# The backward half of the step-weighted C times B, moved from one VectorE multiply to four ScalarE copies per chunk

## The chip, the cores and the metric

The kernel runs on one core of one Trainium2 chip. The metric is the device time of one execution in microseconds (us). TensorE multiplies matrices, VectorE, ScalarE and GpSimd work on tiles in the on-chip memory SBUF and in TensorE's result banks, and the queues of SyncE, ScalarE and GpSimd issue DMA transfers. Each engine works its instructions in order, and engines wait for one another on semaphores.

## The reference

Two layers of a bidirectional encoder over 512 tokens of width 1024. The part that matters here is the Mamba-2 scan, in chunks of 128 tokens, once forward and once backward over the same x, B and C (8 groups, 4 heads each, state 128):

```python
def ssd_chunked(x, dt, A, Bm, Cm):
    ...
    X = (x * dt[..., None]).reshape(b, c, l, g, r, p)
    ...
    Lmat = jnp.exp(jnp.where(lower, seg, -jnp.inf))
    CB = jnp.einsum("bclgn,bcsgn->bcgls", Cc, Bc)
    y_diag = jnp.einsum("bcgrls,bcsgrp->bclgrp", CB[:, :, :, None] * Lmat, X)
    ...
    y_off = jnp.einsum("bclgn,bcgrpn->bclgrp", Cc, prev) * decay_out[..., None]
    return (y_diag + y_off).reshape(b, s, h, p)
...
    y_f = ssd_chunked(xs, dt_f, A[0], Bm, Cm)
    flip = lambda t: jnp.flip(t, axis=1)
    y_b = flip(ssd_chunked(flip(xs), flip(dt_b), A[1], flip(Bm), flip(Cm)))
    y = y_f + y_b + xs.astype(jnp.float32) * d_skip[:, None]
    y = y.reshape(b, s, D_INNER) * jax.nn.silu(z.astype(jnp.float32))
```

Around it stand a combined input projection, a Conformer convolution branch, gates, layer norms and a SwiGLU block, all of them large matrix products.

## The kernel before

Activations lie transposed, 128 features by 512 tokens. Every float32 product is made of three passes on TensorE, over a high and a low part of each operand (lines 855 to 857). All weights come as one stream of tiles of 512 KB in four slots. SyncE loads a tile to `raw`, ScalarE's `hi` (lines 466 and 467) writes its high part to `whi` and its negative to `wlo`, and GpSimd's `lo` (line 354) then issues a DMA that adds the tile itself to `wlo`; TensorE may use the slot when that has landed.

Each layer works its 8 groups in 4 pairs (`pair`), and then runs the dense stages. The order inside a pair is written out by hand, once for each engine. A pair begins with projections and ends with the output projection of its 512 inner features. Between these each of its two groups goes through its four chunks c = 0 to 3:

- GpSimd's `masked_steps` and TensorE's `exponent` make the exponents, ScalarE's `decay` (line 518, eight activations of 128x64) takes them through Exp to `E[:, c]`, forward and backward in one 128x128 matrix for each head.
- TensorE's `c_dot_b` makes C times B of all four chunks. VectorE's `mask_cb` (line 1313) writes it masked to `cb`, the upper and the lower triangle apart (FWD and BWD), and tells with `cb_done`.
- VectorE's `mix` (lines 1351 to 1359) weights `cb` with the steps dt of each head, backward and forward, in `tm`, and multiplies the sum into `E[:, c]`. It tells with `m_ready`.
- TensorE's `state` makes the chunk states, ScalarE's `state` (line 526) copies them to `H` in three parts, state 0, 1 and 2. VectorE's `entering` (lines 1324 and 1327) makes the entering states of them by four carries and four gains; its fourth instruction waits for state 2 (`st_evac`). It tells with `h_ready`.
- ScalarE's `skip` (line 510) starts `y` with x times D.
- TensorE's `y_chunk` multiplies `E[:, c]` with x (line 971), and then, behind the wait for `h_ready`, the states with C (line 977). For chunks 2 and 3 it first waits until VectorE's `outputs` of chunk 0 or 1 has read the banks (line 1379, `yp_read`). `outputs` ends with the gate (line 1383).
- ScalarE's `square`, GpSimd's `group_rms` and VectorE's `normalise_y` (line 1390) normalise y, TensorE's `y_transpose` (line 988) turns it.

Order of VectorE in the second group: `mix` of chunks 0 and 1, `entering`, `mix` 2, `outputs` 0, `mix` 3, `outputs` 1 to 3. TensorE's order behind it: chunk 3 of `y_chunk`, the output projection's first six k-steps (line 855 with `y_hi`; the fifth and sixth use weight slot 1), and then `y_transpose`.

Of the kernel before, what the change touches and what calls it, by code (L numbers as in the profile page):

```python
# [100 lines left out]
def on(cyc, n):  # L101

    return cyc[0] + n, cyc[1] + n


def build(nc, x_in, p_in, w_stream, w_dt, w_ple, par_in, out):
    ctx = ExitStack()
    with ctx:
        def sb(name, shape, dtype=F32, where=None):
            return (where or ctx).enter_context(nc.sbuf_tensor(name, shape, dtype))  # L110

        def sem(name):
            return ctx.enter_context(nc.semaphore(name))
# [27 lines left out]
        with ExitStack() as r:  # L141
            cin = sb("conv_in", [P, 4, T], F32, r)
            feat = sb("xs_b_c", [P, 4, T], F32, r)
            xtok = sb("x_tok", [P, CH, GW], F32, r)
            btok = sb("b_tok", [P, CH, STATE], F32, r)
            ztok = sb("z_tok", [P, 2, T], F32, r)
            E = sb("decay", [P, CH, HG, P], F32, r)
            rhs = sb("seg_rhs", [P, 2, 2 * HG, HB], F32R, r)
            cb = sb("cb_masked", [P, 2, CH, P], F32, r)
            xw = sb("x_weighted", [P, 2, 2, GW], F32, r)  # L150
            H = sb("states", [P, CH * 2, GW], F32, r)
            y = sb("y_tok", [P, CH, GW], F32, r)
            tm = sb("tmp_m", [P, HG, P], F32, r)
            ty = sb("tmp_y", [P, 2, GW], F32, r)
            junk = sb("squares", [P, GW], F32, r)
        with ExitStack() as r:
# [31 lines left out]
        ident = sb("ident", [P, P])  # L188
        par = sb("params", [P, NPAR])
        stepf = steps[:, :, :, :, :].rearrange("p k d c h -> p k (d c h)")  # L190
        tmf = tm[:, :, :].rearrange("p a b -> p (a b)")
        tyf = ty[:, :, :].rearrange("p a b -> p (a b)")
        swap = E[:, 1, 0, :]
        nega = E[:, 1, 1, 0:2 * HEADS]
# [51 lines left out]
        st_done = sem("st_done")  # L246
        st_evac = sem("st_evac")
        h_ready = sem("h_ready")
        m_ready = sem("m_ready")
        yo_done = sem("yo_done")  # L250
        xd_ready = sem("xd_ready")
# [51 lines left out]
        def seen(n):  # L303

            return n + EARLY
# [5 lines left out]
        def open_(e, *ss):  # L311
            for s in ss:
                e.sem_inc(s, EARLY)
# [139 lines left out]

        @block.scalar
        def _(act):
            open_(act, xh_done, silu_done, tok_evac, xd_ready, exp_done, st_evac, ss_done, yh_done,
                  sq_ready, std_ready, zf_ready, zh_ready, bh_done, fh_done,
                  square_ready, off_sq_ready, diag_ready, gate_ready, e_evac, esq_ready, estd_ready, dt_evac, dt_e, cum_exp, nega_e,
                  dtw_hi, *hi_done)
# [29 lines left out]
            def silu(G, c):  # L489
                act.wait_ge(conv_done, seen(4 * G + c + 1))  # L490
                act.activation(feat[:, c, :], feat[:, c, :], ACT.Silu).then_inc(silu_done, 1)
# [12 lines left out]
            def skip(g, G):  # L504

                act.wait_ge(tok_evac, seen(3 * G + 2))
                act.wait_ge(yt_done, seen(2 * G))
                for h in range(HG):
                    e = slice(h * HEAD, (h + 1) * HEAD)
                    i = act.activation(y[:, :, e], xtok[:, :, e], ACT.Copy, scale=par[:, O_DSK + g * HG + h:O_DSK + g * HG + h + 1])  # L510
                i.then_inc(xd_ready, 1)

            def decay(g, G, c):
                act.wait_ge(seg_done, seen(CH * G + c + 1))
                for h in range(HG):
                    for half in range(2):
                        t = slice(half * HB, (half + 1) * HB)
                        i = act.activation(E[:, c, h, t], quarters(bank[4 + c % 2])[:, h, t], ACT.Exp,  # L518
                                           bias=of(EDGE, half, c, g)[:, h:h + 1])
                i.then_inc(exp_done, 1)  # L520

            def state(G, n):

                act.wait_ge(st_done, seen(3 * G + n + 1))
                dst = (H[:, 3:5, :], H[:, 0:6:5, :], H[:, 2:8:5, :])[n]
                act.activation(dst, halves(bank[6 + n % 2]), ACT.Copy).then_inc(st_evac, 1)
# [79 lines left out]
            def pair(L, base, j, first=False):  # L606

                c0 = (base[0] + j * PAIR_CYCLES, base[1] + j * PAIR_BANKS)
                G0 = L * GROUPS + j * 2
                G1 = G0 + 1  # L610
                g0, g1 = 2 * j, 2 * j + 1
                act.wait_ge(conv_done, seen(4 * G0))
                for c in range(4):
                    if first and c == 3:
                        decays(L)
                    conv_input(G0, c, c0, c)
                z_gate(G0, on(c0, 1), 0, 0)
                silu(G0, 0)
                silu(G0, 1)
                z_gate(G0, on(c0, 1), 1, 1)  # L620

                act.wait_ge(conv_done, seen(4 * G0 + 2))
                take(on(c0, 1), 2, cin[:, 0, :])
                xs_tokens(G0, 0)
                xs_tokens(G0, 1)
                silu(G0, 2)
                silu(G0, 3)
                decay(g0, G0, 0)
                hi(on(c0, 2), 2)
                conv_input(G1, 1, on(c0, 1), 3)  # L630
                decay(g0, G0, 1)
                b_tokens(G0)
                skip(g0, G0)
                act.wait_ge(conv_done, seen(4 * G0 + 4))
                conv_input(G1, 2, on(c0, 2), 0)
                decay(g0, G0, 2)
                state(G0, 0)
                take(on(c0, 2), 1, cin[:, 3, :])
                decay(g0, G0, 3)
                state(G0, 1)  # L640
                state(G0, 2)
                hi(on(c0, 3), 1)
                silu(G1, 0)
                silu(G1, 1)
                for c in range(CH):
                    square(G0, c)
                z_gates(G1, on(c0, 2), (2, 3))
                xs_tokens(G1, 0)
                xs_tokens(G1, 1)
                round_y(0, g0, G0, 0)  # L650
                round_y(0, g0, G0, 1)
                silu(G1, 2)
                silu(G1, 3)
                take(on(c0, 3), 1, sg[:, :], ACT.Sigmoid)
                b_tokens(G1)
                decay(g1, G1, 0)
                decay(g1, G1, 1)
                state(G1, 0)
                state(G1, 1)
                hi(on(c0, 4), 0)  # L660
                decay(g1, G1, 2)
                state(G1, 2)
                skip(g1, G1)
                decay(g1, G1, 3)
                hi(on(c0, 4), 1)
                want(3, ACT.Sigmoid)
                hi(on(c0, 4), 2)
                act.wait_ge(evac[0], seen(c0[1] + 4))
                take(on(c0, 3), 3, sg[:, :], ACT.Sigmoid)
                for c in range(CH):  # L670
                    square(G1, c)
                hi(on(c0, 4), 3)
                round_y(1, g1, G1, 0)
                round_y(1, g1, G1, 1)
                for s in range(SLOTS):
                    act.wait_ge(used[1 + s % 2 * 2], seen(c0[1] + 5 + s // 2))
                    hi((c0[0] + 5, c0[1] + 4), s)
# [546 lines left out]
        def _(dve):  # L1224
# [121 lines left out]

            def mix(g, G, c):

                dve.wait_ge(cb_done, seen(G + 1))
                dve.wait_ge(m_ready, seen(CH * G + c))  # L1350
                step(dve.tensor_tensor(tm[:, :, :], cb[:, BWD, c, :].unsqueeze(1).broadcast_to([P, HG, P]),
                                       of(DTK, BWD, c, g).unsqueeze(2).broadcast_to([P, HG, P]), ALU.mult))
                dve.wait_ge(dve_order, issued())
                for h in range(HG):
                    step(dve.scalar_tensor_tensor(out=tm[:, h, :], in0=cb[:, FWD, c, :], scalar=of(DTK, FWD, c, g)[:, h:h + 1],
                                                  in1=tm[:, h, :], op0=ALU.mult, op1=ALU.add))
                dve.wait_ge(dve_order, issued())
                dve.wait_ge(exp_done, seen(CH * G + c + 1))
                dve.tensor_tensor(E[:, c], E[:, c], tm[:, :, :], ALU.mult).then_inc(m_ready, 1)

            def outputs(g, G, c):

# [182 lines left out]
            with dve.Fori(0, LAYERS) as L:  # L1545
# [54 lines left out]
                for j in range(PAIRS):  # L1600
# [8 lines left out]
                    if j > 0:  # L1609
                        long_filter(j - 1, (CONV_A - LATER, CONV_A))  # L1610
                    mask_cb(G0)
                    mix(g0, G0, 0)
                    conv(g1, G1, 0, [(c0 + 1, 2), (c0 + 1, 3)])
                    weighted_xs(g0, G0, 2)
                    mix(g0, G0, 1)
                    entering(g0, G0)
# [11 lines left out]
                    weighted_xs(g1, G1, 0)  # L1628
                    weighted_xs(g1, G1, 1)
                    mask_cb(G1)  # L1630
                    mix(g1, G1, 0)
                    dve.wait_ge(ua_ready, seen(KT * L + 2 * j))
                    glu(c0 + 3, 0, 0)
                    weighted_xs(g1, G1, 2)
                    mix(g1, G1, 1)
                    entering(g1, G1)
# [235 lines left out]
```

## Time and profile before

| | |
|---|---|
| median of 3 runs | 2415.36 us (2410.65 to 2415.5) |
| profiled execution | 2412.09 us, span 2410.5 us |
| mean granted TensorE clock of it | 0.997 |
| a pair | about 142 to 143 us, eight pairs |
| busy share of the span | TensorE 98%, VectorE 63%, ScalarE 57%, GpSimd 24% |

The span is the stretch from the first to the last instruction of the profiled execution. The shares are means over stages of different kinds: VectorE is close to full inside the pairs and mostly waits in the dense stages. Times in the rows below are us from the start of the span, durations in the grouped lists are ns where they say mean.

### The profile page before, as it was taken

The page shows a single profiled execution, that of the slowest core. Times are in us where ns is not written, and L with a number is a line of the kernel's source. Part 1 is how long each engine was busy: PE and PEld are TensorE (multiplying, and loading weights), DVE is VectorE, ACT ScalarE, POOL GpSimd, SP SyncE. Part 2 cuts the span into 40 slices and gives each one's busy share as a digit, 9 for nine tenths or more (in the row PEclk, how much of TensorE's full clock was granted, in tenths as well). Part 3 has the DMA queues.
Part 4 walks back from the last instruction along what each step waited for, and adds up shares of the span by engine and source line. Part 5 has one row for each costly group of instructions (what it writes and reads, how often), then busy time and mean ns, then how long its engine had stood idle before and what let it go on. Part 6 is the DMA issues. An engine that isn't in the chain of part 4 may idle for free.

```text
span 2410.5 us, 35334 instructions
## 1 busy us (share of the span) xinstructions
PE 2369.6 (98%) x11464; PEld 1946.8 (81%) x11464; DVE 1510.7 (63%) x2553; ACT 1371.2 (57%) x2242; POOL 581.7 (24%) x721
## 2 busy tenths in 40 slices
PE   8999999999999999999999999999999999999998
PEld 6878788887877788888788787888878778888876
DVE  5999999999546211113768999999995461111136
ACT  6756656475564644345557466664756656443455
POOL 3423333242111111111124243332421111111110
PEclk9999999999999999999999999999999999999999
DMA  8576585766888789889665857757577868988995
GB/s 213 130 168 147 130 181 112 173 136 153 182 183 194 163 191 194 192 191 214 167 148 120 183 123 159 169 106 174 123 174 175 194 164 186 196 189 194 194 213 139
DMA packets 111173, 406.04 MB, mean 168 GB/s; under 512 B 12337, under 2 KB 12337, under 8 KB 110769
## 3 DMA queue, kind: packets, MB, share of 16 engines
q0 software_dynamic: 54144, 197.16, 49.1%
q1 hardware_dynamic: 55728, 202.66, 25.3%
q10 hardware_dynamic: 1152, 4.37, 0.5%
q8 instruction: 78, 1.28, 0.2%
q14 instruction: 71, 0.57, 0.1%
HBM read 402.04 MB, written 2.10 MB: 168 GB/s over the span
## 4 chain that ended last, share of the span: by engine, by line
PE 88%; DVE 5%; ACT 2%; issue 2%; DMA 2%; POOL 0%; ACTq 0%; POOLq 0%; SPq 0%; DVEq 0%
PE bank L855 24%; PE bank L857 23%; PE bank L856 23%; PE bank L897 3%; PE bank L898 3%; PE bank L900 2%; PE bank L971 2%; DMA w_lo<-w_stream 2%; PE bank L977 1%; PE bank L959 1%; PE bank L1186 1%; PE bank L942 1%; PE bank L943 1%; PE bank L927 1%; PE bank L988 1%
## 5 line engine op out<-in xcount | busy, mean ns | idle before, releaser
L354 POOL DMA_DIRECT2D w_lo<-w_stream x376 | 328.6, 874 | 1594.0 <-ACT w_lo L467 1539.4
L855 PE MATMUL bank<-x_hi,w_hi 128*128 128x512 f32 x1728 | 686.7, 397 | 0.0
L857 PE MATMUL bank<-x_hi,w_lo 128*128 128x512 f32 x1728 | 674.0, 390 | 0.0
L856 PE MATMUL bank<-x_lo,w_hi 128*128 128x512 f32 x1728 | 673.3, 390 | 0.0
L466 ACT ACTIVATE w_hi<-w_raw 128x1024 fp32r<-128x1024 f32 x378 | 403.2, 1067 | 279.9 <-PE bank L857 239.8
L467 ACT ACTIVATE w_lo<-w_raw 128x1024 fp32r<-128x1024 f32 x378 | 400.3, 1059 | 0.0
L855 PEld LDWEIGHTS bank<-x_hi,w_hi 128*128 128x128 f32 x1728 | 324.6, 188 | 68.8 <-issue 3.4
L857 PEld LDWEIGHTS bank<-x_hi,w_lo 128*128 128x128 f32 x1728 | 324.5, 188 | 68.9
L856 PEld LDWEIGHTS bank<-x_lo,w_hi 128*128 128x128 f32 x1728 | 324.8, 188 | 67.9 <-issue 3.3
L1268 DVE SCALAR_TENSOR_TENSOR z_a<-glu_out,params,z_a 128x497 f32<-128x497 f32 (+14 forms) x480 | 321.2, 737 | 0.0
L1726 DVE TENSOR_TENSOR glu_out<-bank,sigmoids 128x512 f32<-128x512 f32 x44 | 30.4, 692 | 416.5 <-PE bank L857 416.5
L364 POOL TENSOR_SCALAR_AFFINE_SELECT seg_rhs<-steps_split 128x512 fp32r<-128x512 f32 (+1 forms) x256 | 218.1, 904 | 70.5 <-PE bank L943 59.9
L1268 DVE SCALAR_TENSOR_TENSOR xs_b_c<-conv_in,params,xs_b_c 128x510 f32<-128x510 f32 (+1 forms) x256 | 206.3, 874 | 0.0
L855 PE MATMUL bank<-act_a_hi,w_hi 128*128 128x512 f32 x480 | 190.4, 397 | 6.5 <-DMA w_lo<-w_stream 6.5
L857 PE MATMUL bank<-act_a_hi,w_lo 128*128 128x512 f32 x480 | 188.5, 393 | 0.0
L856 PE MATMUL bank<-act_a_lo,w_hi 128*128 128x512 f32 x480 | 187.3, 390 | 0.0
L897 PE MATMUL bank<-w_hi,x_hi 128*128 128x256 f32 x512 | 153.1, 299 | 0.9 <-issue 0.8
L898 PE MATMUL bank<-w_lo,x_hi 128*128 128x256 f32 x512 | 144.9, 283 | 0.0
L900 PE MATMUL bank<-w_hi,x_lo 128*128 128x256 f32 x496 | 140.3, 283 | 0.0
L518 ACT ACTIVATE decay<-bank,steps 128x64 f32<-128x64 f32 x512 | 113.8, 393 | 0.2
L855 PEld LDWEIGHTS bank<-act_a_hi,w_hi 128*128 128x128 f32 x480 | 90.2, 188 | 29.2 <-issue 6.2
L532 ACT ACTIVATE squares<-y_tok 128x256 f32<-128x256 f32 x64 | 26.6, 416 | 148.5 <-DVE y_tok L1383 148.5
(245 smaller groups left out, 3662.8 us busy)
## 6 DMA issues: line engine op xcount, KB each, us to landing
w_raw<-w_stream SPq DMA_DIRECT2D x378, 512.0 KB, 5.0
w_lo<-w_stream POOLq DMA_DIRECT2D x376, 512.0 KB, 7.5
z_b<-x_in SPq DMA_DIRECT2D x4, 512.0 KB, 7.1
w_ple_in<-w_ple ACTq DMA_DIRECT2D x2, 1024.0 KB, 11.5
out<-z_b SPq DMA_DIRECT2D x4, 512.0 KB, 5.0
ple_p<-p_in ACTq DMA_DIRECT2D x2, 512.0 KB, 6.5
params<-par_in ACTq DMA_DIRECT2D x2, 340.0 KB, 3.9
tmp_m<-w_dt ACTq DMA_DIRECT2D x2, 256.0 KB, 5.0
```

The costliest lines, as they stand in the source:

```text
L354: gp.dma_start(wlo[:, s, :], w_stream[cyc, s].bitcast(F32R), accum_op=ALU.add).then_inc(lo_done[s], 16)
L364: i = gp.affine_select(out=rhs[0:rows, part], in_=ad, compare_op=ALU.is_ge, fill=0.0, base=base, pattern=[[0, 2 * HG], [sign, HB]], channe ...
L466: act.activation(whi[:, s, :], raw[:, s % 2, :], ACT.Copy)
L467: act.activation(wlo[:, s, :], raw[:, s % 2, :], ACT.Copy, scale=-1.0).then_inc(hi_done[s], 1)
L518: i = act.activation(E[:, c, h, t], quarters(bank[4 + c % 2])[:, h, t], ACT.Exp, bias=of(EDGE, half, c, g)[:, h:h + 1])
L855: pe.matmul(dst, wh, mh, start=first, stop=False)
L856: pe.matmul(dst, wh, ml, start=False, stop=False)
L857: return pe.matmul(dst, wl, mh, start=False, stop=last)
L897: pe.matmul(dst, xh[:, k, t], h, start=k == 0, stop=False)
L898: pe.matmul(dst, xh[:, k, t], l, start=False, stop=False)
L900: pe.matmul(dst, xl[:, k, t], h, start=False, stop=end)
L1268: q = dve.scalar_tensor_tensor(out=outs[i][:, a:b], in0=ins[i][:, a + o:b + o], scalar=w[:, k:k + 1], in1=outs[i][:, a:b], op0=ALU.mult, o ...
```

## The change

ScalarE gets a function `backward`. For one chunk it makes the backward product, cb times dt, by one copy with a scale for each of the four heads (128x128 each) into one of two halves of `tm`, and tells with `back_ready`. It waits for `cb_done`, and for the product that used this half two chunks ago. VectorE's `mix` loses its multiply (line 1351) and its wait for the chunk before, and waits for `back_ready` instead; the four multiply-adds for the forward half and the product stay. In ScalarE's order the calls stand at eight places of a pair, and `want(4, ACT.Exp)` in the second group makes the table load of the exponentials come ahead of the first of them. In VectorE's order `mix` of chunk 0 moves behind the next group's first convolution (first group) and behind the first `glu` (second group).

```diff
-            tm = sb("tmp_m", [P, HG, P], F32, r)
+            tm = sb("tmp_m", [P, 2, HG, P], F32, r)
...
+            def backward(g, G, c):
+
+                act.wait_ge(cb_done, seen(G + 1))
+                act.wait_ge(m_ready, seen(CH * G + c - 1))
+                for h in range(HG):
+                    i = act.activation(tm[:, c % 2, h, :], cb[:, BWD, c, :], ACT.Copy, scale=of(DTK, BWD, c, g)[:, h:h + 1])
+                i.then_inc(back_ready, 1)
...
                 skip(g0, G0)
+                backward(g0, G0, 0)
+                backward(g0, G0, 1)
...
                 state(G0, 2)
+                backward(g0, G0, 2)
                 hi(on(c0, 3), 1)
                 silu(G1, 0)
                 silu(G1, 1)
+                backward(g0, G0, 3)
...
                 b_tokens(G1)
+                want(4, ACT.Exp)
+                backward(g1, G1, 0)
                 decay(g1, G1, 0)
                 decay(g1, G1, 1)
+                backward(g1, G1, 1)
                 state(G1, 0)
                 state(G1, 1)
                 hi(on(c0, 4), 0)
+                backward(g1, G1, 2)
                 decay(g1, G1, 2)
                 state(G1, 2)
                 skip(g1, G1)
                 decay(g1, G1, 3)
+                backward(g1, G1, 3)
...
             def mix(g, G, c):
 
+                t = tm[:, c % 2]
                 dve.wait_ge(cb_done, seen(G + 1))
-                dve.wait_ge(m_ready, seen(CH * G + c))
-                step(dve.tensor_tensor(tm[:, :, :], cb[:, BWD, c, :].unsqueeze(1).broadcast_to([P, HG, P]),
-                                       of(DTK, BWD, c, g).unsqueeze(2).broadcast_to([P, HG, P]), ALU.mult))
-                dve.wait_ge(dve_order, issued())
+                dve.wait_ge(back_ready, seen(CH * G + c + 1))
                 for h in range(HG):
-                    step(dve.scalar_tensor_tensor(out=tm[:, h, :], in0=cb[:, FWD, c, :], scalar=of(DTK, FWD, c, g)[:, h:h + 1],
-                                                  in1=tm[:, h, :], op0=ALU.mult, op1=ALU.add))
+                    step(dve.scalar_tensor_tensor(out=t[:, h, :], in0=cb[:, FWD, c, :], scalar=of(DTK, FWD, c, g)[:, h:h + 1],
+                                                  in1=t[:, h, :], op0=ALU.mult, op1=ALU.add))
...
                     mask_cb(G0)
+                    conv(g1, G1, 0, [(c0 + 1, 2), (c0 + 1, 3)])
                     mix(g0, G0, 0)
-                    conv(g1, G1, 0, [(c0 + 1, 2), (c0 + 1, 3)])
...
                     mask_cb(G1)
-                    mix(g1, G1, 0)
                     dve.wait_ge(ua_ready, seen(KT * L + 2 * j))
                     glu(c0 + 3, 0, 0)
+                    mix(g1, G1, 0)
```

ScalarE's row in the second group of a pair stood so before, from `b_tokens` (`b_tok`) to the second `hi` (`w_hi`, `w_lo`):

```order
L502 ACTIVATE b_tok<-bank 128x512
L518 ACT_TABLE_LOAD
L518 ACTIVATE decay<-bank,steps 128x64 x16
...
L526 ACTIVATE states<-bank 128x512
...
L526 ACTIVATE states<-bank 128x2x256
...
L466 ACTIVATE w_hi<-w_raw 128x1024
L467 ACTIVATE w_lo<-w_raw 128x1024
L518 ACTIVATE decay<-bank,steps 128x64 x8
...
L526 ACTIVATE states<-bank 128x2x256
...
L510 ACTIVATE y_tok<-x_tok,params 128x4x64 x4
L518 ACTIVATE decay<-bank,steps 128x64 x8
L466 ACTIVATE w_hi<-w_raw 128x1024
```

The same place in the changed kernel, whose lines are numbered a little differently, from the table load on:

```order
L591 ACT_TABLE_LOAD
L591 ACTIVATE spare<-eps 128x1
...
L528 ACTIVATE tmp_m<-cb_masked,steps 128x128 x4
L519 ACTIVATE decay<-bank,steps 128x64 x16
L528 ACTIVATE tmp_m<-cb_masked,steps 128x128 x4
...
L528 ACTIVATE tmp_m<-cb_masked,steps 128x128 x4
L519 ACTIVATE decay<-bank,steps 128x64 x8
...
L535 ACTIVATE states<-bank 128x2x256
...
L511 ACTIVATE y_tok<-x_tok,params 128x4x64 x4
L519 ACTIVATE decay<-bank,steps 128x64 x8
L528 ACTIVATE tmp_m<-cb_masked,steps 128x128 x4
L467 ACTIVATE w_hi<-w_raw 128x1024
```

Three calls of `backward`, of four copies each, now stand ahead of the last copy of `states` (state 2), and four ahead of the weight split behind them.

VectorE's row from `mask_cb` to `entering`, in the second group, before:

```order
L1313 TENSOR_TENSOR cb_masked<-bank,tri_ge 128x512
...
L1351 TENSOR_TENSOR tmp_m<-cb_masked,steps 128x512
L1355 SCALAR_TENSOR_TENSOR tmp_m<-cb_masked,steps,tmp_m 128x128 x4
...
L1359 TENSOR_TENSOR decay<-decay,tmp_m 128x512
...
L1410 TENSOR_TENSOR glu_out<-bank,sigmoids 128x512
...
L1303 TENSOR_TENSOR x_weighted<-x_tok,steps 128x256 x2
L1351 TENSOR_TENSOR tmp_m<-cb_masked,steps 128x512
L1355 SCALAR_TENSOR_TENSOR tmp_m<-cb_masked,steps,tmp_m 128x128 x4
...
L1359 TENSOR_TENSOR decay<-decay,tmp_m 128x512
L1324 TENSOR_TENSOR tmp_y<-states,steps 128x256 x2
```

And in the changed kernel:

```order
L1331 TENSOR_TENSOR cb_masked<-bank,tri_ge 128x512
...
L1426 TENSOR_TENSOR glu_out<-bank,sigmoids 128x512
...
L1371 SCALAR_TENSOR_TENSOR tmp_m<-cb_masked,steps,tmp_m 128x128 x4
L1375 TENSOR_TENSOR decay<-decay,tmp_m 128x512
...
L1321 TENSOR_TENSOR x_weighted<-x_tok,steps 128x256 x2
...
L1371 SCALAR_TENSOR_TENSOR tmp_m<-cb_masked,steps,tmp_m 128x128 x4
L1375 TENSOR_TENSOR decay<-decay,tmp_m 128x512
L1342 TENSOR_TENSOR tmp_y<-states,steps 128x256 x2
```

The multiply is gone from each chunk, and the `glu` stands ahead of the first `mix`.

## Rows read from the trace of the kernel before

**Rows 1.** The page: busy us (share of the span), and the chain that ended last.

```profile
PE 2369.6 (98%) x11464; PEld 1946.8 (81%) x11464; DVE 1510.7 (63%) x2553; ACT 1371.2 (57%) x2242; POOL 581.7 (24%) x721
...
PE 88%; DVE 5%; ACT 2%; issue 2%; DMA 2%; POOL 0%; ACTq 0%; POOLq 0%; SPq 0%; DVEq 0%
```

**Rows 2.** Waits on TensorE: us in total, times, longest us.

```profile
PE bank L971 <- DVE tmp_y L1379: 11.1, 8, 1.5
```

**Rows 3.** Busy us by stage; PEclk is the granted clock.

```profile
core 0: us, PE busy (x) PEld busy (x) DVE busy (x) ACT busy (x) POOL busy (x), PEclk, DMA share, GB/s
...
202.00:288.00 86.00, 83.61 (x472) 70.03 (x470) 81.67 (x157) 61.89 (x145) 35.80 (x47) 1.00 0.60 131
344.00:430.00 86.00, 84.53 (x472) 71.39 (x471) 81.01 (x156) 61.77 (x145) 35.67 (x47) 0.98 0.61 129
...
421.90:425.20 3.30, 3.30 (x10) 2.69 (x10) 3.09 (x8) 1.02 (x4) 0.01 (x1) 0.50 1.01 243
```

**Rows 4.** Timeline of TensorE, layer 0, third pair: start, us, instruction, idle before.

```profile
412.68 0.70 PE L977 MATMUL bank<-states,xs_b_c 128*128 128x256 f32 x2
...
418.54 1.08 PE L977 MATMUL bank<-states,xs_b_c 128*128 128x512 f32 x2
421.09 1.26 PE L971 MATMUL bank<-x_tok,decay 128*128 128x64 f32 x8 [1.47 <-DVE tmp_y L1379]
...
428.26 1.04 PE L988 MATMUL bank<-ident,y_tok 128*128 128x128 f32 x8
```

**Rows 5.** Timeline of VectorE, same pair, second group.

```profile
401.40 1.13 DVE L1351 TENSOR_TENSOR tmp_m<-cb_masked,steps 128x512 f32<-128x512 f32 x1
...
409.86 0.75 DVE L1324 TENSOR_TENSOR tmp_y<-states,steps 128x256 f32<-128x256 f32 x2
...
411.88 0.75 DVE L1327 TENSOR_TENSOR states<-states,tmp_y 128x256 f32<-128x256 f32 x2
412.55 0.68 DVE L1351 TENSOR_TENSOR tmp_m<-cb_masked,steps 128x512 f32<-128x512 f32 x1
413.27 1.14 DVE L1355 SCALAR_TENSOR_TENSOR tmp_m<-cb_masked,steps,tmp_m 128x128 f32<-128x128 f32 x4
...
420.52 0.42 DVE L1379 TENSOR_TENSOR tmp_y<-tmp_y,bank 128x256 f32<-128x256 f32 x1
```

**Rows 6.** Timeline of TensorE, second pair, around the same place.

```profile
278.71 1.08 PE L971 MATMUL bank<-x_tok,decay 128*128 128x64 f32 x8 [1.46 <-DVE tmp_y L1379]
...
282.91 0.40 PE L855 MATMUL bank<-y_hi,w_hi 128*128 128x512 f32 x1
...
285.35 1.09 PE L988 MATMUL bank<-ident,y_tok 128*128 128x128 f32 x8 [0.87 <-DVE y_tok L1390]
```

**Rows 7.** Timeline of ScalarE, third pair, second group.

```profile
401.42 3.38 ACT L518 ACTIVATE decay<-bank,steps 128x64 f32<-128x64 f32 x16
...
408.99 0.80 ACT L526 ACTIVATE states<-bank 128x512 f32<-128x512 f32 x1
409.47 1.91 ACT L510 ACTIVATE y_tok<-x_tok,params 128x256 f32<-128x256 f32 x4
411.07 1.94 ACT L518 ACTIVATE decay<-bank,steps 128x64 f32<-128x64 f32 x8
412.63 1.32 ACT L466 ACTIVATE w_hi<-w_raw 128x1024 fp32r<-128x1024 f32 x1
```

**Rows 8.** Groups by line and form: busy us, mean ns, idle before.

```profile
L1351 DVE TENSOR_TENSOR tmp_m<-cb_masked,steps 128x512 f32<-128x512 f32 x64 | 50.5, 789 | 0.6
...
L577 ACT ACTIVATE glu_out<-ident,token_rstd 128x128 f32<-128x128 f32 x16 | 5.1, 390 | 1.9 <-DVE token_rstd L1522 1.9
```

**Rows 9.** The chain in order of time: start us, us, what.

```profile
776.73 1.29 ACT glu_out L577 x4
```

**Rows 10.** Timeline of ScalarE, third pair, first group, its first `square`.

```profile
377.42 0.42 ACT L532 ACTIVATE squares<-y_tok 128x256 f32<-128x256 f32 x1 [4.73 <-DVE y_tok L1383]
```

**Rows 11.** Timeline of GpSimd: the DMA issue for slot 1.

```profile
415.61 0.86 POOL L354 DMA_DIRECT2D w_lo<-w_stream  x1 [6.32 <-ACT w_lo L467]
```

**Rows 12.** The page's DMA issues: KB each, median us to landing.

```profile
w_lo<-w_stream POOLq DMA_DIRECT2D x376, 512.0 KB, 7.5
```

More of the change, by code:

```diff
@@ L190, in build @@
         stepf = steps[:, :, :, :, :].rearrange("p k d c h -> p k (d c h)")
-        tmf = tm[:, :, :].rearrange("p a b -> p (a b)")
+        tmf = tm[:, 0].rearrange("p a b -> p (a b)")
         tyf = ty[:, :, :].rearrange("p a b -> p (a b)")
@@ L248, in build @@
         h_ready = sem("h_ready")
+        back_ready = sem("back_ready")
         m_ready = sem("m_ready")
@@ L455, in _ @@
         def _(act):
-            open_(act, xh_done, silu_done, tok_evac, xd_ready, exp_done, st_evac, ss_done, yh_done,
+            open_(act, xh_done, silu_done, tok_evac, xd_ready, back_ready, exp_done, st_evac, ss_done, yh_done,
                   sq_ready, std_ready, zf_ready, zh_ready, bh_done, fh_done,
@@ L1347, in mix @@
             def mix(g, G, c):
+                t = tm[:, c % 2]
                 dve.wait_ge(cb_done, seen(G + 1))
-                dve.wait_ge(m_ready, seen(CH * G + c))
-                step(dve.tensor_tensor(tm[:, :, :], cb[:, BWD, c, :].unsqueeze(1).broadcast_to([P, HG, P]),
-                                       of(DTK, BWD, c, g).unsqueeze(2).broadcast_to([P, HG, P]), ALU.mult))
-                dve.wait_ge(dve_order, issued())
+                dve.wait_ge(back_ready, seen(CH * G + c + 1))
                 for h in range(HG):
-                    step(dve.scalar_tensor_tensor(out=tm[:, h, :], in0=cb[:, FWD, c, :], scalar=of(DTK, FWD, c, g)[:, h:h + 1],
-                                                  in1=tm[:, h, :], op0=ALU.mult, op1=ALU.add))
+                    step(dve.scalar_tensor_tensor(out=t[:, h, :], in0=cb[:, FWD, c, :], scalar=of(DTK, FWD, c, g)[:, h:h + 1],
+                                                  in1=t[:, h, :], op0=ALU.mult, op1=ALU.add))
                 dve.wait_ge(dve_order, issued())
                 dve.wait_ge(exp_done, seen(CH * G + c + 1))
-                dve.tensor_tensor(E[:, c], E[:, c], tm[:, :, :], ALU.mult).then_inc(m_ready, 1)
+                dve.tensor_tensor(E[:, c], E[:, c], t, ALU.mult).then_inc(m_ready, 1)
             def outputs(g, G, c):
```

## The prediction

> **What bounds the kernel now.** The first view is the page: TensorE is busy 98% of the span, and it holds 88% of the chain that ended last; VectorE has 5% of it and ScalarE 2% [rows 1]. So VectorE's or ScalarE's time counts only where TensorE waits for it. The second view is the list of waits on TensorE: the matmuls of line 971 (`y_chunk`) waited 11.1 us for `tmp_y` of line 1379 (`outputs`), 8 times [rows 2]. Eight is once in each pair. The third view is busy time by stage: in the 86 us of a pair in which its two groups are worked VectorE is busy 81.0 us and ScalarE 61.8 [rows 3]. VectorE is nearly full there and ScalarE has room, so the move looks right on the averages. But these 86 us are not one stretch, and the timeline has to say where the room lies.
>
> In the pair shown (the third of layer 0), chunk 3 of the second group starts on TensorE at 421.09, after matmuls that began at 418.54 and last about 0.7 us in effect: some 1.8 us lost, of which 1.47 is put down as a wait [rows 4]. What it waits for is the second `outputs`, whose line 1379 ends at 420.94 [rows 5]. The next gate is `y_transpose` at 428.26, set by `normalise_y` two steps behind the same chain. After the wait the granted clock was 0.50 from 421.9 to 425.2, the 1.2 GHz level [rows 3]. In the pair before it stayed at 1.00, and there chunk 3 to `y_transpose` took 6.64 us (278.71 to 285.35), with 0.87 of it waited, against 7.17 us here [rows 4, 6]. So a clock drop costs 0.5 us net, since part of it fills that wait. Of the eight pairs' windows four show 0.98, as the second row of [rows 3], and four 1.00, as the first: four drops.
>
> VectorE runs without a gap from 401.40 to 420.94. Yet ScalarE does too: from 401.42 to beyond 412.63 its rows follow one another without a wait [rows 5, 7]. In this stretch the kernel has no free engine to move work to.
>
> **Removed.** 64 multiplies of 128x512 on VectorE, 789 ns each, 50.5 us in all [rows 8]; uncontended, the next instruction follows after 0.72 us (412.55 to 413.27). In the second group that would be 2.9 us off the chain to the wait, and 0.4 more at chunk 0, where the multiply took 1.13 us [rows 5].
>
> **Added.** 256 ScalarE copies of 128x128 with a scale read from a tile. The same form stands in the trace at line 577: 390 ns each [rows 8], four in 1.29 us [rows 9], so a step of 0.30 and 1.21 us for four. That row has form, function and memory alike, so I take it. Bounds from the timeline: the 64-column decays step by 0.20 (eight from 411.07 to 412.63), the 256-column skips by 0.40 (four from 409.47 to 411.07), hence 0.8 to 1.6 us for four [rows 7]. In all 77 us go onto ScalarE for 50 off VectorE. The small activation (`want`) only pulls the table load forward, and costs 0.1 us per pair.
>
> The Trainium skill speaks against this change: ScalarE: Activation LUTs, section Rules for kernel authors, puts plain multiplications on VectorE, not on ScalarE. The trace agrees on the price, 1.21 us against 0.72 for one chunk. By that rule alone every chunk would lose the difference, 64 x 0.49 = 31 us; by the rows only those lose for which ScalarE has no gap, and they lose by its queue.
>
> **First group.** ScalarE gets two copies of four behind `skip`, one behind the states, one behind the SiLUs: 4.9 us. Behind them it had 4.73 us idle before its first `square` [rows 10], and a smaller gap before that, and the four chunks' products are wanted late: cover enough. VectorE comes out ahead, but the second group starts at `mask_cb`, which waits for TensorE. So what is won in the first group can't be carried over: cost and gain nothing. If the cover were gone, `outputs` of chunk 0 would be late next.
>
> **Second group, ScalarE's queue.** In front of state 2 (408.99, ends 409.79) now stand backward 0, 1 and 2 and `want`: 3 x 1.21 + 0.1 = 3.73 us. State 2 ends at 413.5. VectorE's `entering` needs it for its fourth instruction, and the trace had it there just in time (entering begins at 409.86). VectorE itself can't use its saving there: it now waits for backward 0 and 1. Behind the wait stand five instructions of 0.336 us [rows 5]: `h_ready` comes at 415.3 instead of 412.63. TensorE waits for it at 412.68 [rows 4], so a new wait of up to 2.6 us opens in chunk 0.
>
> From `h_ready` to the end of line 1379 in the second `outputs` were 8.31 us (412.63 to 420.94); two multiplies less make it 6.88, so it ends at 422.2 and chunk 3 starts at 422.35: **1.25 us later than before**. The rest of ScalarE is in time for this. Decay 2 ends at 412.7. `skip` ends at 411.07 + 3.73 = 414.8, and is wanted by the first `outputs`, four multiply-adds and a product (1.9 us) behind `h_ready`, at 417.2. Backward 3 ends at 412.63 + 4.95 = 417.6, and is wanted another 1.7 us later, at 418.9. Everything behind on VectorE moves with it, and `y_transpose` could start at about 428.98.
>
> **The weights behind it.** The split of slot 1 for the projection (412.63) moves by 4 x 1.21 + 0.1 = 4.95 us, and with it GpSimd's issue of `w_lo`, from 415.61 to 420.56 [rows 11]; the landing is 7.5 us behind the issue in the median [rows 12]: 428.1. TensorE wants it for the fifth k-step behind chunk 3, 4.20 us after it [rows 6]: 426.55. It then has 1.4 us to do before `y_transpose`: 429.4, perhaps 429.0 where the landing is quick. Against 427.73 (no clock drop) or 428.26 (with one) that is 1.3 to 1.7 or 0.8 to 1.1 us per pair.
>
> **Sum.** Four pairs at 1.5 and four at 1.0: **10 us slower**. The profiled execution took 2412.1 us, 3.3 under the median of the three runs, 2415.4, and inside them. 2422 on its own time, 2425 on the median; I say 2423.
>
> **Rivals.**
> *The wait moves nowhere and VectorE's saving counts (faster).* If ScalarE's copies were cheap or early enough, the 1.8 us wait and the 0.87 us wait go, 2.7 us per pair, and the four drops at 0.5: 24 us, 2388. It decides at state 2: the times balance when it is late by 1.25 us less, 2.45 us, or 0.8 us per four copies, which is just the lower bound. For it speaks that VectorE is full; against, that ScalarE has no gap there. Chance 0.12.
> *A draw.* Copies at 0.9 to 1.0 us for four, or a landing and drops that cost nothing more, give 0 to +4.8 us. The change doesn't do what it says, if you like: it trades one wait for another. Chance 0.23.
> *More of it (slower).* At 0.40 per copy the state is late by 4.9 and chunk 3 by 2.45 us; the weights by 6.5: 2.9 us per pair, 2435. Or the clock: now TensorE waits twice close together, about 2.6 and 0.7 us. If every pair drops after it at the price seen between the levels (3.3 us at half is 1.65 us, not filled by a wait any more), that is 8 x 1.65 on top of 10, less what is in it: 2433. The Trainium skill, TensorE: Matmul & The Clock Gate, section What's actually happening, says that throttled is the default state and that activity releases the clock. By that rule, more idle time makes more drops; the trace agrees in kind (the drop follows the wait) but shows equal waits with and without one. Chance together 0.2. The plain forecast, +5 to +15, has 0.45.
>
> **How the numbers follow.** A measurement of this kernel tells about 0.2%, 4.8 us, from no change. Slower by more: 0.45 + 0.2 = 0.65; same 0.23; faster 0.12. The range leaves out the faster rival and the far end: 2412 to 2436. If only the likeliest case is right, 2418 to 2429.
>
> **What would show it.** In the profile after: no line 1351; 256 copies on ScalarE near 0.39 us; VectorE idle some 2.5 us in each `entering` of a second group, ended by ScalarE's `states`; a TensorE wait for `states` in chunk 0 of the second group, eight times, that was not there; a smaller wait on line 1379; a wait for `w_lo` at the projection of slot 1; first groups without new waits. I am wrong if state 2 ends before 412.3 in that frame, if the copies step by 0.2, or if clock drops vanish.

## The result: 0.9% slower, by twice the sum

| | us, median | lowest to highest | granted clock of the runs |
|---|---|---|---|
| before | 2414.0 (4 runs) | 2410.65 to 2415.5 | profiled run 0.997 |
| after | 2433.32 (4 runs) | 2428.22 to 2443.74 | 0.988 to 0.995 |

The ratio is 1.0092, 95% interval 1.0072 to 1.0111: 19.3 us slower where 10 were forecast. The median lies inside the stated range (2412 to 2436) and outside its likeliest part (2418 to 2429). The profiled execution of after is its slowest run (2443.74, span 2442.1), and some 12 us of its difference to the profile of before lie outside the second groups. There its granted clock was 0.50 in four stretches (from 16.8, 498.0, 1170.5 and 2382.2, together 20.5 us) where before had none but at its very end; at half speed that is about 10 of the 12 us, an estimate. What brought these four no run shows. Two executions far off all others (4801.39 us of `before + 8 copies`, 3370.55 us of the kernel before, run beside the last two kernels) are left out of the medians below.

The page of after, and its chain that ended last:

```profile
PE 2392.1 (98%) x11464; PEld 1958.2 (80%) x11464; DVE 1444.1 (59%) x2489; ACT 1445.3 (59%) x2506; POOL 591.8 (24%) x721
...
PE 80%; ACT 8%; DVE 4%; DMA 4%; issue 3%; POOL 1%; ACTq 0%; POOLq 0%; SPq 0%; DVEq 0%
```

VectorE is 67 us less busy and ScalarE 74 more [rows 1]. That looks like a fair trade, and it tells nothing of the time. The list of waits on TensorE does (us in total, times, longest us; y_chunk is L989 and L995 now, y_transpose L1006, the projection L873):

```profile
PE bank L989 <- ACT states L535: 10.3, 8, 1.4
PE bank L873 <- DMA w_lo<-w_stream: 8.8, 10, 2.3
PE bank L873 <- DVE x_lo L1421: 7.5, 2, 6.9
PE bank L995 <- DVE states L1345: 5.1, 8, 0.6
PE bank L1006 <- DVE y_tok L1406: 3.7, 8, 0.5
```

The wait of [rows 2] (line 1379, now 1395) is gone in all eight pairs. Two new ones, once per pair each, stand in its place, at chunk 0: for state 2, and for VectorE's entering states behind it. The copies of `backward`, and one of the two places where VectorE now waits (the other is state 2, in its timeline below), in the groups by line and form:

```profile
L528 ACT ACTIVATE tmp_m<-cb_masked,steps 128x128 f32<-128x128 f32 x256 | 85.8, 484 | 0.0
L1371 DVE SCALAR_TENSOR_TENSOR tmp_m<-cb_masked,steps,tmp_m 128x128 f32<-128x128 f32 x256 | 81.4, 378 | 15.5 <-ACT tmp_m L528 15.5
```

The same pair as in [rows 4, 5, 7], timeline of ScalarE. The row `spare` is the one that pulls the table load forward:

```profile
406.29 0.20 ACT L591 ACTIVATE spare<-eps 128x1 f32<-128x1 f32 x1
406.40 1.27 ACT L528 ACTIVATE tmp_m<-cb_masked,steps 128x128 f32<-128x128 f32 x4
407.57 3.36 ACT L519 ACTIVATE decay<-bank,steps 128x64 f32<-128x64 f32 x16
410.72 1.37 ACT L528 ACTIVATE tmp_m<-cb_masked,steps 128x128 f32<-128x128 f32 x4
...
414.75 1.37 ACT L528 ACTIVATE tmp_m<-cb_masked,steps 128x128 f32<-128x128 f32 x4
415.92 1.84 ACT L519 ACTIVATE decay<-bank,steps 128x64 f32<-128x64 f32 x8
417.49 0.76 ACT L535 ACTIVATE states<-bank 128x512 f32<-128x512 f32 x1
...
419.56 1.91 ACT L519 ACTIVATE decay<-bank,steps 128x64 f32<-128x64 f32 x8
421.13 1.49 ACT L528 ACTIVATE tmp_m<-cb_masked,steps 128x128 f32<-128x128 f32 x4
422.30 1.26 ACT L467 ACTIVATE w_hi<-w_raw 128x1024 fp32r<-128x1024 f32 x1
```

Three calls of four copies, 1.17 us each, stand ahead of state 2 (417.49). The timeline of VectorE:

```profile
418.28 0.42 DVE L1345 TENSOR_TENSOR states<-states,tmp_y 128x256 f32<-128x256 f32 x1 [2.66 <-ACT states L535]
418.62 0.75 DVE L1342 TENSOR_TENSOR tmp_y<-states,steps 128x256 f32<-128x256 f32 x2
419.29 0.75 DVE L1345 TENSOR_TENSOR states<-states,tmp_y 128x256 f32<-128x256 f32 x2
...
426.39 0.42 DVE L1395 TENSOR_TENSOR tmp_y<-tmp_y,bank 128x256 f32<-128x256 f32 x1
...
430.09 0.69 DVE L1385 TENSOR_TENSOR tmp_y<-bank,steps 128x512 f32<-128x512 f32 x1 [2.36 <-PE bank L995]
```

And the timeline of TensorE, with its busy time by stage below it (columns as in [rows 3], PEclk the third last):

```profile
418.39 1.08 PE L989 MATMUL bank<-x_tok,decay 128*128 128x64 f32 x8 [1.34 <-ACT states L535]
420.10 1.22 PE L995 MATMUL bank<-states,xs_b_c 128*128 128x256 f32 x2 [0.63 <-DVE states L1345]
421.11 1.81 PE L989 MATMUL bank<-x_tok,decay 128*128 128x64 f32 x8
422.71 2.02 PE L995 MATMUL bank<-states,xs_b_c 128*128 128x512 f32 x2
...
429.89 1.00 PE L989 MATMUL bank<-x_tok,decay 128*128 128x64 f32 x8
```

```profile
418.39:419.50 1.11, 1.07 (x8) 0.94 (x8) 1.11 (x4) 1.11 (x4) 0.00 (x0) 1.00 1.10 170
419.60:426.20 6.60, 6.10 (x16) 4.54 (x17) 6.39 (x18) 6.57 (x18) 0.86 (x1) 0.50 0.29 57
426.50:430.00 3.50, 3.50 (x20) 2.69 (x18) 1.17 (x3) 2.92 (x7) 0.86 (x1) 1.00 0.91 172
```

Read the last two together with VectorE. TensorE waits in chunk 0, and for 6.6 us from then on it works at 0.50, the 1.2 GHz level, as in [rows 3] but for twice as long. VectorE has read chunk 1's banks at 426.8. TensorE comes to chunk 3 only at 429.89, and it is VectorE that waits now, 2.36 us, for TensorE's chunk 2.

All kernels below are compared on one measure: how much later TensorE starts each piece of work in the second groups than in the trace of before, summed over the eight pairs, from the first group's `y_transpose` on. The columns are chunk 0, 1, 2, 3 and the `y_transpose` behind (each what is added there), their sum, the pairs in whose second group the clock fell, and the difference of the medians. The first five columns, the sum and the drops are those of the one profiled execution. The rows are, in this order, the kernels before, after, `e2`, `e1`, `e3`, `f5`, `d4`, `d8`, `d12`, `e4`, `f1`, `f2`, `f3` and `f4` of the experiments.

```
kernel                        c0     c1     c2     c3   y_tr    sum  drops  median
before                         -      -      -      -      -      -      4       -
after                       13.4    9.0   15.7  -12.4   -5.9   19.7      8   +19.3
second group alone          13.3    8.9   17.5  -12.4   -5.9   21.2      8   +16.9
first group alone            0.0    0.1    0.0    0.7    0.7    1.5      4    +3.5
all, state 2 ahead           4.0    6.9   20.7  -12.4   -1.6   17.7      6   +11.9
all, state 2, decay 3 ahead  4.2    7.0   -0.1   -2.8    0.5    8.7      0   +10.0
before + 4 copies            0.0    0.9    1.3   -0.8   -2.1   -0.6      0    +0.1
before + 8 copies            4.4    6.9    4.3   -3.7   -2.2    9.8      2   +10.8
before + 12 copies          15.1    9.6   15.6  -11.0   -4.6   24.7      7   +24.7
chunks 2, 3                 -0.1    0.1    2.3  -12.4   -0.8  -11.0      0   -12.7
chunks 2, 3, no first group  0.0   -0.1    2.3  -12.4    0.5   -9.7      0    -7.7
chunk 3                      0.6    0.5    0.0   -5.8   -2.0   -6.7      0    -6.6
chunks 2, 3, split ahead     0.1    0.1   43.9  -12.4   -5.9   25.7      8   +24.9
chunks 2, 3, decay 3 ahead   0.1    0.0    0.0  -11.1    2.6   -8.4      1    -9.6
```

### The profile page after: what moved, and what is told of

The parts are those of the page before. It is cut to its first block, busy times and chain, and to the rows that moved or that the text cites. A ratio compares the mean times of both kernels' runs of the same rounds, so it can differ in the third digit from the quotient of the medians.

```text
span 2442.1 us, 35599 instructions
## 1 busy us (share of the span) xinstructions
PE 2392.1 (98%) x11464; PEld 1958.2 (80%) x11464; DVE 1444.1 (59%) x2489; ACT 1445.3 (59%) x2506; POOL 591.8 (24%) x721
## 4 chain that ended last, share of the span: by engine, by line
PE 80%; ACT 8%; DVE 4%; DMA 4%; issue 3%; POOL 1%; ACTq 0%; POOLq 0%; SPq 0%; DVEq 0%
PE bank L873 21%; PE bank L875 21%; PE bank L874 21%; PE bank L915 2%; PE bank L916 2%; PE bank L918 2%; PE bank L995 2%; PE bank L989 2%; DMA w_lo<-w_stream 2%; DMA w_raw<-w_stream 2%; ACT decay L519 2%; ACT w_lo L468 1%; ACT tmp_m L528 1%; PE bank L1204 1%; ACT w_hi L467 1%
## 5 line engine op out<-in xcount | busy, mean ns | idle before, releaser
L873 PE MATMUL bank<-x_hi,w_hi 128*128 128x512 f32 x1728 | 692.3, 401 | 3.6 <-DMA w_lo<-w_stream 3.6
L873 PEld LDWEIGHTS bank<-x_hi,w_hi 128*128 128x128 f32 x1728 | 327.1, 189 | 75.4 <-issue 8.3
L365 POOL TENSOR_SCALAR_AFFINE_SELECT seg_rhs<-steps_split 128x512 fp32r<-128x512 f32 (+1 forms) x256 | 228.6, 947 | 80.7 <-PE bank L961 70.2
L873 PE MATMUL bank<-act_a_hi,w_hi 128*128 128x512 f32 x480 | 190.4, 397 | 5.2 <-DMA w_lo<-w_stream 5.2
L873 PEld LDWEIGHTS bank<-act_a_hi,w_hi 128*128 128x128 f32 x480 | 90.2, 188 | 28.5 <-issue 6.7
L473 ACT ACTIVATE sigmoids<-bank 128x512 f32<-128x512 f32 x88 | 52.3, 594 | 101.1 <-PE bank L875 94.5
```

Source lines behind the costliest of these rows:

```text
L365: i = gp.affine_select(out=rhs[0:rows, part], in_=ad, compare_op=ALU.is_ge, fill=0.0, base=base, pattern=[[0, 2 * HG], [sign, HB]], channe ...
L873: pe.matmul(dst, wh, mh, start=first, stop=False)
```

## The experiments

Theory A at the outset: the loss is made in the second group, where ScalarE has no gap; state 2 comes late, TensorE waits in chunk 0, and its clock falls behind that wait. The rivals: the first group costs too; VectorE's new waits for `tmp_m` cost by themselves; the weight split costs.

### One group at a time

`e1_first_group` makes only the first group's chunks on ScalarE, `e2_second_group` only the second's; the other group is VectorE's again.

```diff
 def backward(g, G, c):
+    if c not in ON_ACT[g % 2]:     # ([0,1,2,3], []) or ([], [0,1,2,3])
+        return
```

> Only the first group of each pair has its backward half on ScalarE; the second group's mix multiplies on VectorE as before and stands ahead of glu as before. Theory A (the loss is made in the second group alone, by state 2 being late on ScalarE and by the clock drops behind the wait): no change, 2411 to 2418, chunk 3 of the second group waits for line 1379 as before, four or so clock drops. Rival B (the added ScalarE work and the moved first-group order cost by themselves, 39 us of copies): about half of the loss, 2422 to 2426.

> Only the second group has its backward half on ScalarE, with want and glu placed as in the changed kernel; the first group is as before. A: the whole loss, 2430 to 2436, a TensorE wait for states in each of eight pairs and a clock drop behind each. B: half of it, 2422 to 2426.

Measured: 2416.63 (ratio 1.0009, 1.0000 to 1.0018) and 2430.06 (1.0063, 1.0048 to 1.0077), against 2413.18. In the first group TensorE's intervals are as before to 0.01 us. Most of the loss, 16.9 of 19.3 us, is the second group's. The 3.5 us of the first group alone are not settled: their interval just reaches no change, and its trace shows no cost in the first groups. The six runs of `e2` show also the part that the clock has in it, without any change of the kernel: granted 0.998 and 0.996, 2423.4 twice; at 0.996, 2427.7; at 0.993, 0.991 and 0.990, 2432.4, 2432.4 and 2433.1.

### State 2 ahead

```diff
 hi(on(c0, 4), 0)
-backward(g1, G1, 2)
 decay(g1, G1, 2)
 state(G1, 2)
+backward(g1, G1, 2)
```

> The changed kernel with one call moved: in the second group backward of chunk 2 stands behind decay 2 and state 2 instead of ahead of them, the same work on every engine. A: state 2 is 1.2 us earlier, so TensorE's two waits in chunk 0 shrink from some 2.3 to 1.1 us and with them the loss: 2416 to 2425, fewer clock drops. If the loss came from the amount of ScalarE work or from backward 3 and the weight split behind it (rival), it stays at 2430 to 2436.

Measured: 2425.07 (1.0052, 1.0039 to 1.0065). Chunk 0's delay falls from 13.4 to 4.0 us, as it should, by 9.4, but the loss by 7.4 only, from 19.3 to 11.9. A wait that was not there stands in chunk 1, here in the waits on TensorE and then in its timeline, third pair:

```profile
PE bank L995 <- ACT decay L519: 9.0, 8, 1.1
```

```profile
422.23 1.83 PE L995 MATMUL bank<-states,xs_b_c 128*128 128x512 f32 x2 [1.13 <-ACT decay L519]
```

### The price of a wait for state 2 alone

The kernel before, in which ScalarE makes 4, 8 or 12 copies of 128x128 into a buffer that nobody reads, ahead of decay 2 and state 2 of the second group. VectorE keeps all its work.

```diff
 hi(on(c0, 4), 0)
+extra(4, L * PAIRS + j)     # 8, 12
 decay(g1, G1, 2)
 state(G1, 2)
```

> The kernel before, plus four ScalarE copies of 128x128 with a scale from a tile, in the second group ahead of decay 2; VectorE keeps all its work, and the copies' results are used by nobody. State 2 gets late by about 1.2 us. Theory A: it lands at 411.0 in the frame of the third pair, where VectorE wants it at 410.9: within 3 us of before. A theory by which ScalarE's work as such costs would have 8 x 1.2 = 10 us more.

> The same with eight copies, state 2 late by about 2.5 us. A: h_ready and line 1379 are 1.4 us later and TensorE's chunk 0 waits some 1.4 us: 8 x 1.4 = 11 us, and up to 1.65 us in each pair whose clock drops in addition: 2425 to 2438. ScalarE's work as such: 8 x 2.5 = 20 us at once, and double of the first step.

> The same with twelve copies, state 2 late by about 3.8 us, as in the changed kernel, but with VectorE's multiplies still there. A: h_ready 2.7 us later, line 1379 as well: 8 x 2.7 = 22 us and clock drops: 2436 to 2450, more than the changed kernel, since there VectorE's chain is 1.4 us shorter.

Measured: 2412.66 (0.9999, 0.9988 to 1.0010), 2423.33 (1.0043, 1.0030 to 1.0055) and 2437.25 (1.0097, 1.0079 to 1.0116), against 2412.57. The first four are free, the next four cost 10.7 us and the last four 13.9. Eight pairs by the 1.17 us of four copies are 9.4; the rest is probably the clock's, which falls in 0, 2 and 7 of the pairs. The change puts 12 copies there too, and loses 19.3 where this one loses 24.7: that goes with VectorE's freed time, but was not taken apart. One thing speaks against a simple rule: with four copies chunk 3 still waits 1.31 us for line 1379, nearly as before, and no pair's clock falls.

### Only the chunks for which ScalarE has time

`e4_late_chunks` keeps chunks 0 and 1 of the second group on VectorE, and makes 2 and 3 on ScalarE behind state 2.

```diff
-ON_ACT = ([0, 1, 2, 3], [0, 1, 2, 3])
+ON_ACT = ([0, 1, 2, 3], [2, 3])
...
 decay(g1, G1, 2)
 state(G1, 2)
+backward(g1, G1, 2)
 skip(g1, G1)
 decay(g1, G1, 3)
 backward(g1, G1, 3)
```

> First group on ScalarE in full; in the second group only chunks 2 and 3, both behind state 2; chunks 0 and 1 are multiplied on VectorE as before, and glu and the table load stand as before. A: state 2 is on time, two multiplies (1.4 us) go off the chain to line 1379, and chunk 3 waits some 0.4 us instead of 1.8; no clock drops in the pairs. 2401 to 2410, faster than before. If the weight split of slot 1, 2.4 us later, binds (rival), a wait for w_lo takes the gain: 2412 to 2418.

Measured: 2400.45 (0.9953, 0.9940 to 0.9966), faster than both kernels. All waits on TensorE in its trace:

```profile
PE bank L876 <- DMA w_lo<-w_stream: 16.4, 15, 1.8
PE bank L876 <- DVE x_lo L1431: 7.3, 2, 7.0
PE bank L1040 <- ACT glu_out L590: 2.1, 4, 0.5
PE bank L1192 <- DVE rstd L1701: 1.2, 2, 0.6
PE bank L876 <- issue: 0.2, 1, 0.2
```

No wait for VectorE or ScalarE is left in the groups, and no drop of the clock in a pair. What is new is `w_lo`, 16.4 us against 6.5 before. Of these 7.9 us lie in the second groups, once per pair, 0.6 to 1.4 us between chunk 3 and `y_transpose`, where before there were none; two backwards stand ahead of the split of slot 1. In the third pair:

```profile
423.02 0.50 PE L876 MATMUL bank<-y_hi,w_hi 128*128 128x512 f32 x1 [1.02 <-DMA w_lo<-w_stream]
```

### How much of it, and which gate is next

`f1_late_chunks_alone` has the first group back on VectorE; `f2_last_chunk` only chunk 3 of the second on ScalarE.

> Of the second group chunks 2 and 3 are made on ScalarE behind state 2, as in the version that ran in 2400; the first group is all VectorE's, as before the change. Theory A (all gain and loss arise in the second group, between state 2 and chunk 3): the same 11 to 12 us below the kernel before, 2401, the wait of TensorE on line 1379 gone, no clock drops. Rival (the first group's freed VectorE time is part of that gain, through conv and the glu that start earlier): 2404 to 2410, with chunk 3 waiting in part again.

> Of the second group only chunk 3 is made on ScalarE; the first group all four. One multiply less (0.72 us uncontended) ahead of line 1379's wait of 1.47. Theory A: the wait falls to about 0.75 us in each pair; if a drop of the clock follows any wait, some drops stay; 2414 less 8 x 0.75 = 6, so about 2408. The wait for w_lo at the projection is lengthened by one backward instead of two, some 0.6 us per pair. Rival (a wait below a certain length costs nothing, and all of the gain of the two-chunk version comes from the clock): 2401 as that one.

Measured, against 2413.45: 2405.79 (0.9962, 0.9949 to 0.9975) and 2406.82 (0.9972, 0.9961 to 0.9982). The interval of the first overlaps that of the version with the first group (0.9940 to 0.9966). Its time lies where the rival had it (2404 to 2410) and not at theory A's 2401, but the wait in chunk 3 that the rival wanted is not there: the first four columns are the same within 0.2 us. So 7.7 us are won by the two late chunks alone; whether the first group adds the other 5 is not settled. In the second, the wait at chunk 3 is 0.8 us at the longest, 5.3 in all against 11.1: one multiply's time, 0.72 us, is one step of the gain, and no pair's clock falls.

`f3_split_ahead` was to win the waits for `w_lo` back:

```diff
 state(G1, 2)
 backward(g1, G1, 2)
-skip(g1, G1)
-decay(g1, G1, 3)
 backward(g1, G1, 3)
 hi(on(c0, 4), 1)
+skip(g1, G1)
+decay(g1, G1, 3)
```

> As the version with chunks 2 and 3 of the second group and the whole first group on ScalarE, which ran in 2400, but the backward of chunk 3 comes right behind that of chunk 2, and the weight split of slot 1 behind it, ahead of skip and of the last decay. That version's trace shows 16.4 us of TensorE waits for w_lo (15 times) against 6.5 (6 times) before the change. By the rows of its third pair skip would end at 413.3 where it is wanted at 413.27, the last decay at 414.9 where it is wanted at 415.24, so nothing else gets late, and the split ends 3 us earlier. Theory A: the w_lo waits of the pairs go, 1.2 us per pair, and the time falls to about 2391. Rival 1 (the landing of w_lo is set by the DMA queues and not by the split): 2400 as before. Rival 2 (skip or the decay come late and chunk 2 or 3 waits again): 2403 to 2410.

Measured: 2438.34 (1.0113, 1.0095 to 1.0132): a miss by 47 us. `w_lo`'s waits are back at 5.7 us, none of them in a second group, as expected. But TensorE waits in chunk 1, in the list of waits and in the timeline of the third pair:

```profile
PE bank L998 <- ACT decay L521: 25.2, 8, 3.2
```

```profile
423.55 2.04 PE L998 MATMUL bank<-states,xs_b_c 128*128 128x512 f32 x2 [3.15 <-ACT decay L521]
```

I had asked only when VectorE wants the last decay. TensorE wants it earlier: chunk 1's product of states and C goes into the bank that holds the exponents of that decay, and `y_chunk` waits for it (`exp_done`, c + 3). In the trace of before the decay's eight activations start at 411.07 and end at 413.0, and TensorE comes at 414.06: 1.05 us to spare. That would explain three results: 1.13 us in state 2 ahead; 3.15 here; and the 2.3 us at chunk 2 in e4, 0.28 in each pair, where backward 2 puts 1.17 us ahead of the decay (that is 0.12 more than the 1.05 to spare, so the size is only roughly met). Call this theory B. Two kernels test it, with the decay ahead of `skip` in e4, and with state 2 and the decay ahead of backward 2 in the full change:

```diff
 state(G1, 2)
-skip(g1, G1)
 decay(g1, G1, 3)
+backward(g1, G1, 2)     # f5 only
+skip(g1, G1)
 backward(g1, G1, 3)
```

> As the version with chunks 2 and 3 of the second group and the whole first group on ScalarE (2400), but with the last decay ahead of skip. In the version with the weight split ahead TensorE waited 25.2 us, 8 times, in chunk 1 for that decay: the second matmul of chunk 1 writes the bank that the decay reads. In the 2400 version chunk 1 to chunk 2 is 0.28 us longer than before the change in each pair (backward 2 ahead of the decay takes 1.17, the decay had 1.05 to spare). Theory B (the last decay is a gate for TensorE in chunk 1): these 0.28 go, 2.3 us in all, 2398, and no new wait, since skip has time. Rival (the 0.28 comes from elsewhere, or skip is late then): 2400 to 2405, with the 0.28 still in the intervals or a wait on skip.

> All eight chunks on ScalarE as in the change, but in the second group state 2 and the last decay both stand ahead of backward 2, and skip behind it. The version with only state 2 ahead took 2425, its trace has 9.0 us of waits of TensorE on the last decay in chunk 1 (8 times 1.13) and drops of the clock behind them. Theory B: those waits go; what stays of the cost are chunk 0's 0.5 and 0.9 us per pair from backward 0 and 1 ahead of entering, against 1.6 won at chunk 3, and 5 us of waits for w_lo: about 2412 to 2414, if the clock drops go with the long wait. Rival (every wait in chunk 0 brings a drop of the clock, whatever its length): 8 x 1.6 more, 2425. Rival (backward 2, now later, makes mix 2 late, and chunk 2 or 3 waits for VectorE): 2418 or more with a wait on line 1395 or for decay L1375.

Measured, against 2413.58: 2404.03 (0.9954, 0.9941 to 0.9967) and 2423.56 (1.0052, 1.0038 to 1.0067). Both times miss what theory B said for them, 2398 and 2412 to 2414. The column of chunk 2 goes to 0.0 and to -0.1, so theory B holds for the gate in both. It is worth nothing in the time: in f4 the 2.3 us come back as `w_lo` waits (10.8 us for 7.9 in the second groups) and a later chunk 3. In f5 no pair's clock falls any more, yet the last rival came true. The waits on TensorE:

```profile
PE bank L873 <- DMA w_lo<-w_stream: 17.1, 15, 2.6
PE bank L989 <- DVE tmp_y L1395: 8.4, 8, 1.1
PE bank L873 <- DVE x_lo L1421: 8.2, 2, 7.0
PE bank L995 <- DVE states L1345: 5.1, 8, 0.6
```

Line 1395's wait is back, and on VectorE `mix` 2 waits 1.03 us for backward 2 in the third pair. It loses 10.0 us, as much as the prediction's sum, with the clock undisturbed in all eight pairs, but not by the prediction's way: state 2 is late here by two calls of `backward` and not three (chunk 0's delay is 4.2 us and not 13.4), and `w_lo` costs 8.8 us in the second groups, once per pair. So it does not measure the change without its clock.

## Why the size was off

Times of after are put into the frame of before by the start of C times B in the third pair, 403.86 against 398.99 in the same view of TensorE: 4.87 us less.

- **The copies.** Forecast 1.21 us for four; measured 1.17 until the next instruction. Right, though one copy shows 484 ns in the mean, and not the 0.39 us named among the signs.
- **State 2.** Forecast to end at 413.5; 418.25 less 4.87 is 413.4. `h_ready` forecast for 415.3; TensorE's matmul behind it starts at 420.10, 415.2. Right. I had put all of TensorE's wait there; 1.34 us of it lies a step earlier, since `y_chunk` wants state 2 already before its first matmul of chunk 0. The whole is as forecast: 415.23 against 412.68 is 2.55 us.
- **Line 1379.** Forecast to end at 422.2; 426.81 less 4.87 is 421.9. Right. The conclusion "chunk 3 starts at 422.35: 1.25 us later than before" is the step that failed. TensorE started chunk 3 at 425.0, 3.9 us later than before, three us after the banks were free. It was not waiting for VectorE any more; it was itself late, at half clock for 6.6 us. The sum can be redone from these rows, as an estimate: before, TensorE was ready for chunk 3 at 419.24 (418.54 and 0.7); 2.55 us of new wait make it 421.8, just when the banks come free, so that nothing is left to wait for; the 6.6 us at half clock then add 3.3 in full, 425.1.
- **The sum.** "Four pairs at 1.5 and four at 1.0" kept the four drops of before at their price of 0.5. Measured: eight drops, five of 3.4 us and three of 6.8. They begin behind chunk 0's waits, ahead of chunk 3: before, the drop lay behind chunk 3's wait and ran into `y_transpose`'s. So the profiled pairs lost 2.5 us each and not 1.25. How much of the loss is the late state and how much the clock is told best by the runs of e2: 10 to 14.5 us at 0.996 to 0.998, near the clock of before, and 19 to 20 us at 0.990 to 0.993. By these the clock has up to half of it. That was my rival "or the clock", 2433, as the median came out; its reason (a longer wait and a second one close to it) was seen, and given too little chance. That its figure is met so closely is in part luck: it priced every drop at 1.65 us, and three of the eight were twice as long, while `y_transpose` took 5.9 us less behind chunk 3 in all.
- **The weights.** The split of slot 1 was forecast for 417.58, and stood at 422.30 less 4.87, 417.4. The wait behind it did not come in after: none of its `w_lo` waits lies in a second group, and chunk 3 was itself 3.9 us late in the pair shown. The 0.4 us per pair that it had added to the sum (429.4 for 428.98) were thus not there. The wait came where TensorE was less late: 7.9 us in the second groups of e4, 8.8 in those of f5, about 1 us per pair.
- **First group: nothing.** Right by the trace; the time of e1, 1.0009 (1.0000 to 1.0018), leaves up to 4 us open.
- **The rival "faster".** Not for this change. In e4 the first of its two waits goes (chunk 3 gains 12.4 us), the place of the second is taken by `w_lo`, and 12.7 of its 24 us are won.

The Trainium skill, TensorE: Matmul & The Clock Gate, section What's actually happening, has it that the slow clock is the default and activity releases it. Kind and order agree here: over the kernels, 0 of 8 pairs drop in e4, where TensorE waits in a second group only for `w_lo`, at most 1.4 us, and all 8 in f3, where it waits 3.15 us for the decay. The length of the wait does not settle it alone (1.47 us, four pairs of eight; 1.31 us with four copies, none).

What stays open is which of two equal pairs drops. The time of f5 was not lowered by its absent drops below that of state 2 ahead (2423.56 and 2425.07, intervals that overlap), whose best run, at clock 1.0, took 2421.63. So the share of the clock is seen in the runs of e2, which differ in nothing else that the record shows, not as a constant per drop.

## What to carry to other kernels

Before work is moved to an engine with a low mean share, look at its rows in the stretch where the other is full: here both were full at once, and only the piece behind ScalarE's last urgent output (state 2) had room, which gave -7.7 us alone, and -12.7 with the first group's chunks too, instead of +19.3. For every instruction that is pushed back list all its readers, those too that only want its source bank free. And price a new wait on TensorE by where it stands: here a loss forecast at 1.25 us per pair became 2.5, because the new wait used up the slack ahead of chunk 3 and the half-clock stretch behind it then counted in full.

## What the runs showed of the hardware

The copy of 128x128 with a scale from a tile shows 484 ns in the mean where the form at line 577 shows 390 [rows 8], yet a call of four takes the engine 1.17 us, less than the 1.21 worked out from line 577. Where instructions of an engine overlap, the mean of one is no price; the step to the next start is.

Four idle copies per pair on ScalarE left the time the same and changed the clock: the profiled run of `d4_copies` has a granted clock of 1.00 over the span, though chunk 3 waits nearly as long as before (10.3 us in all against 11.1 [rows 2]) and `y_transpose` longer (7.1 against 3.5). TensorE's starts in chunks 1 and 2 move there by 0.1 and 0.2 us, no more. What decides between a drop and none at such equal waits no run here shows.
